# Twelve sums of token quarters moved from VectorE to GpSimd, with new slots for weight pieces and a new order in the first up iteration

## The reference

```
def conv_ffn(x, norm_g, w_up, conv_w, conv_b, w_down):
    h = rms_norm(x, norm_g)
    a, b = split(h @ w_up, 2, axis=-1)            # D_FF = 2816 columns each
    a = causal depthwise conv of width 3 over a, + conv_b
    return (silu(a) * b) @ w_down
...
for l in range(2):
    x = x + hybrid_mixer(x, ...)
    x = x + conv_ffn(x, ...)
return rms_norm(x, final_norm)
```

## Time and profile before

| | |
|---|---|
| median of three executions | 1598.31 us |
| profiled execution, its own time | 1598.63 us |
| its span, first to last instruction | 1596.8 us |
| TensorE matmul busy | 1581.9 us (99%) |
| TensorE weight load busy | 1399.0 us (88%) |
| VectorE busy | 1123.5 us (70%) |
| ScalarE busy | 741.4 us (46%) |
| GpSimd busy | 239.7 us (15%) |

### The profile page before, as it was taken

One profiled execution on the slowest core, in us unless ns is written; L12 is line 12 of the kernel. 1 busy time (PEld: TensorE's weight loads), 2 busy tenths in 40 slices (PEclk: granted clock), 3 DMA queues, 4 the chain that ended last, 5 costly groups with the idle time before them and its releaser, 6 DMA issues.

```text
span 1596.8 us, 22779 instructions
## 1 busy us (share of the span) xinstructions
PE 1581.9 (99%) x9174; PEld 1399.0 (88%) x9174; DVE 1123.5 (70%) x1252; ACT 741.4 (46%) x945; POOL 239.7 (15%) x253
## 2 busy tenths in 40 slices
PE   9999999999999999999999999999999999999998
PEld 7888888888888999999988888888888889999887
DVE  7267875785679787796873778658757887888422
ACT  5344334542356555653533533345423555556313
POOL 4000000000221222331330000000004102222120
PEclk9999999999999999999999999999999999999999
DMA  5342222223228788899223322221223488884222
GB/s 193 105 120 79 80 80 92 67 70 101 95 92 245 232 235 234 273 230 260 75 99 105 107 80 79 80 93 67 80 93 105 125 245 220 240 234 145 93 92 93
DMA packets 62308, 216.74 MB, mean 136 GB/s; under 512 B 6912, under 2 KB 7424, under 8 KB 62208
## 3 DMA queue, kind: packets, MB, share of 16 engines
q1 hardware_dynamic: 51408, 180.05, 33.0%
q0 software_dynamic: 8640, 30.41, 10.7%
q10 hardware_dynamic: 2160, 4.86, 1.1%
HBM read 211.10 MB, written 2.10 MB: 134 GB/s over the span
## 4 chain that ended last, share of the span: by engine, by line
PE 97%; DMA 2%; DVE 1%; issue 0%; ACT 0%; DVEq 0%
PE ps L1778 19%; PE ps L1780 19%; PE ps L1779 19%; PE ps L1784 11%; PE ps L1786 11%; PE ps L1785 11%; PE ps L1907 1%; PE ps L1896 1%; DMA w_raw<-wts 1%; PE ps L1874 1%; PE ps L1878 1%; DMA far_raw<-wdn 1%; PE ps L2031 0%; PE ps L1918 0%; PE ps L1844 0%
## 5 line engine op out<-in xcount | busy, mean ns | idle before, releaser
L1201 DVE TENSOR_TENSOR w_lo<-w_raw,w_hi 128x1024 fp32r<-128x1024 f32 x180 | 236.2, 1323 | 131.9 <-ACT w_hi L769 131.4
L1778 PE MATMUL ps<-u_hi,w_hi 128*128 128x512 f32 x768 | 301.5, 393 | 0.0
L1780 PE MATMUL ps<-u_hi,w_lo 128*128 128x512 f32 x768 | 299.2, 390 | 0.0
L1779 PE MATMUL ps<-u_lo,w_hi 128*128 128x512 f32 x768 | 299.1, 390 | 0.0
L769 ACT ACTIVATE w_hi<-w_raw 128x1024 fp32r<-128x1024 f32 x180 | 187.5, 1053 | 150.5 <-DMA w_raw<-wts 144.3
L1784 PE MATMUL ps<-comb_hi,far_hi 128*128 128x256 f32 x688 | 195.1, 284 | 4.1 <-DVE comb_lo L1411 2.4
L1785 PE MATMUL ps<-comb_lo,far_hi 128*128 128x256 f32 x688 | 194.7, 283 | 0.0
L1786 PE MATMUL ps<-comb_hi,far_lo 128*128 128x256 f32 x624 | 176.5, 283 | 0.0
L1780 PEld LDWEIGHTS ps<-u_hi,w_lo 128*128 128x128 f32 x768 | 144.2, 188 | 30.5
L1778 PEld LDWEIGHTS ps<-u_hi,w_hi 128*128 128x128 f32 x768 | 144.4, 188 | 28.4
L1779 PEld LDWEIGHTS ps<-u_lo,w_hi 128*128 128x128 f32 x768 | 144.4, 188 | 28.3
(11 more groups left out here) (311 smaller groups left out, 3294.7 us busy)
## 6 DMA issues: line engine op xcount, KB each, us to landing
w_raw<-wts SPq DMA_DIRECT2D x234, 512.0 KB, 3.5
far_raw<-wts SPq DMA_DIRECT2D x56, 512.0 KB, 3.7
w_raw<-wts POOLq DMA_DIRECT2D x18, 512.0 KB, 10.0
far_raw<-wts POOLq DMA_DIRECT2D x16, 512.0 KB, 7.0
t_raw<-wdn POOLq DMA_DIRECT2D x15, 512.0 KB, 9.9
w_raw<-wdn SPq DMA_DIRECT2D x11, 512.0 KB, 7.6
far_raw<-wdn SPq DMA_DIRECT2D x9, 512.0 KB, 7.4
first_raw<-wts SPq DMA_DIRECT2D x8, 512.0 KB, 6.4
```

What stands on the lines that cost most here:

```text
L1201: nc.vector.tensor_tensor(w_lo[:, s, :], w_raw[:, s, :], w_hi[:, s, :].bitcast(F32), ALU.subtract).then_inc(s_lo, 1)
L1778: nc.tensor.matmul(dst, a_hi, b_hi, start=start, stop=False)
L1779: nc.tensor.matmul(dst, a_hi, b_lo, start=False, stop=False)
L1780: return nc.tensor.matmul(dst, a_lo, b_hi, start=False, stop=stop)
```

## The change

- The twelve chunk_sum operations move from VectorE's program to GpSimd's, between the accumulating transfers: sums 3 to 8 (products 1 and 2) within the two rounds of add_piece for products 2 and 6, sums 12 to 14 (product 4) behind them and ahead of product 4's transfers, sums 15 to 17 (product 5) last. Their waits stay the same.
- RAW_SLOT is new from piece 19 on: product 3 takes slots 0, 2, FAR, FAR+1, FAR+2, FAR+3, and the following go round all eight slots in that manner. The order of SP's loads follows from it, and the waits of u_high for the last far slots are one piece earlier.
- In the first up iteration (n = 0, both layers): SP loads piece 5 behind pieces 2 and 6; ScalarE's last plain_tap moves from ahead of part_high 3 to behind part_high 4; VectorE's last plain_out moves from the end of the plain part to behind part_low(0, 2); its L1702 (now bottom_right) moves ahead of c11 and of part_low(1, 0).

```diff
--- before.py
+++ after.py
@@ -61,8 +61,8 @@
 CHUNKS = 21
 FAR = RING
 RAW_SLOT = [3, 1, 0, 2, FAR, FAR + 1, FAR + 2, FAR + 3, 3, 1, FAR + 2, FAR + 3, 3, 1, FAR + 2, FAR + 3, 3, 1,
-            0, FAR + 2, FAR + 3, 3, 1, 0, 2, FAR, FAR + 1, FAR + 2, FAR + 3, 3, 1, 0, 2, FAR, FAR + 1, FAR + 2,
-            FAR + 3, FAR, FAR + 1, FAR + 2, FAR + 3, FAR]
+            0, 2, FAR, FAR + 1, FAR + 2, FAR + 3, 3, 1, 0, 2, FAR, FAR + 1, FAR + 2, FAR + 3, 3, 1, 0, 2,
+            FAR, FAR + 1, FAR + 2, FAR + 3, FAR, FAR + 1]
 HI_SLOT = [(2, 1, 0, FAR, FAR + 1, FAR + 2, FAR + 3, 3)[u % 8] for u in range(39)] + [FAR, FAR + 1, 3]
 HI_AFTER = (0, 1, 2, 3, 4, 5, 6, 7)
 SUM_K = (1, 2, 4, 5)
@@ -585,10 +585,10 @@
                 load_part(l, 0, 3, W21, s_el[3])
                 sp.wait_ge(s_free, base + 2)
                 load_part(l, 0, 0, W11, s_el[0])
-                load_part(l, 0, 5, W22, s_el[5])
                 sp.wait_ge(s_free, base + 3)
                 load_part(l, 0, 2, W22, s_el[2])
                 load_part(l, 0, 6, W21, s_el6[0])
+                load_part(l, 0, 5, W22, s_el[5])
                 sp.wait_ge(s_free, base + 4)
                 load_part(l, 1, 1, W11, s_el1[1])
                 for n in range(SPLIT if l + 1 == DEPTH else SPLIT - 1):
@@ -703,12 +703,37 @@
                     pool.wait_ge(s_tland[int(j > 1)], l * (32 + 32 * (j > 1)) + 32 + 32 * (j > 1))
                     add_piece(l, j, W12)
 
+            def chunk_sum(l, c):
+
+                k, i = divmod(c, 3)
+                if k == 1:
+                    pool.wait_ge(s_gf, l * FT + HF + 4 * i + chunk(i))
+                    nc.gpsimd.tensor_tensor(chunk_raw(1, i), token_part(1, 1, i), token_part(0, 1, i), ALU.subtract).then_inc(s_csum, 1)
+                if k == 2:
+                    pool.wait_ge(s_csum, l * 12 + i + 1)
+                    pool.wait_ge(s_clo, l * CHUNKS + 3 + i + 1)
+                    nc.gpsimd.tensor_tensor(chunk_raw(2, i), chunk_raw(1, i), token_part(0, 0, i), ALU.add).then_inc(s_csum, 1)
+                if k == 4:
+                    pool.wait_ge(s_csum, l * 12 + i + 1)
+                    nc.gpsimd.tensor_tensor(chunk_raw(4, i), chunk_raw(4, i), token_part(0, 0, i), ALU.subtract).then_inc(s_csum, 1)
+                if k == 5:
+                    pool.wait_ge(s_csum, l * 12 + 3 + i + 1)
+                    pool.wait_ge(s_clo, l * CHUNKS + 6 + i + 1)
+                    nc.gpsimd.tensor_tensor(chunk_raw(5, i), chunk_raw(2, i), token_part(1, 0, i), ALU.subtract).then_inc(s_csum, 1)
+
             def further_sums(l):
 
+                chunk_sum(l, 3)
                 for k, quarter in ((1, W22), (2, W21)):
                     for j in range(PIECES):
+                        if k == 1 and j % 2 == 1:
+                            chunk_sum(l, 4 + j // 2)
+                        if k == 2 and j in (0, 2):
+                            chunk_sum(l, 7 + j // 2)
                         pool.wait_ge(s_qlo, l * UNITS_DOWN + k * PIECES + j + 1)
                         add_piece(l, j, quarter)
+                for c in (12, 13, 14):
+                    chunk_sum(l, c)
                 for j in range(PIECES):
                     u = 4 * PIECES + j
                     s = RAW_SLOT[u]
@@ -758,6 +783,8 @@
                 gated(l, SPLIT - 1)
                 if l + 1 < DEPTH:
                     further_sums(l)
+                    for c in (15, 16, 17):
+                        chunk_sum(l, c)
             sum_squares(DEPTH * 30, lambda k: DEPTH * TILES + k + 1, range(4))
 
         @block.scalar
@@ -956,7 +983,7 @@
                     act.wait_ge(s_tile, down_tile(l - 1) + 6)
                     for k in range(4, KT):
                         if k % 2 == 0:
-                            act.wait_ge(s_unit, (l - 1) * UNITS_DOWN + (40 if k == 4 else 41))
+                            act.wait_ge(s_unit, (l - 1) * UNITS_DOWN + (39 if k == 4 else 40))
                         u_high(k, pcol(l, PAR_ATTN + k))
                         if k % 2 == 1:
                             split_hi(l, k // 2 - 1)
@@ -1086,7 +1113,6 @@
                     done = 7 * (l * SPLIT + n)
                     if n == 0:
                         part_high(l, 0, 2)
-                        plain_tap(l, PLAIN - 1, 1)
                     else:
                         last_quarter(l, n - 1)
                         for h in range(2):
@@ -1097,6 +1123,8 @@
                         act.wait_ge(s_c11, l * SPLIT + n)
                     nc.scalar.activation(copy_x[:], half_tiles(banks(n)[0]), ACT.Copy).then_inc(s_cpx, 1)
                     part_high(l, n, 4)
+                    if n == 0:
+                        plain_tap(l, PLAIN - 1, 1)
                     act.wait_ge(s_prod, done + 2)
                     if n > 0:
                         act.wait_ge(s_c22, l * SPLIT + n)
@@ -1366,6 +1394,14 @@
                 dve.wait_ge(s_el6[n % 2], 16 * (l * ((SPLIT + 1 - n % 2) // 2) + n // 2 + 1))
                 nc.vector.tensor_tensor(part_raw(l, n, 6), part_raw(l, n, 6), part_raw(l, n, 2), ALU.add).then_inc(s_sum4, 1)
 
+            def bottom_right(l, n):
+
+                m = l * SPLIT + n
+                dve.wait_ge(s_prod, 7 * m + 5)
+                dve.wait_ge(s_cpy, m + 1)
+                dve.wait_ge(s_gf, l * FT + 2 * (PLAIN + n))
+                nc.vector.tensor_tensor(cb[:, :, S // 2:S], half_tiles(banks(n)[0]), copy_y[:], ALU.subtract).then_inc(s_c22, 1)
+
             def plain_out(l, g, h):
 
                 slab_done(l, UP0 + 4 * g + 2 * h + 1)
@@ -1409,24 +1445,6 @@
                     nc.vector.scalar_tensor_tensor(out=lo, in0=raw, scalar=-1.0, in1=hi, op0=ALU.mult, op1=ALU.subtract).then_inc(s_clo, 1)
                 else:
                     nc.vector.tensor_tensor(lo, raw, hi, ALU.subtract).then_inc(s_clo, 1)
-
-            def chunk_sum(l, c):
...
             def take_product(l, k):
 
@@ -1662,7 +1680,6 @@
                         if (g, j) == (1, 3):
                             third_sum(l, 0)
                             part_low(l, 0, 1)
-                            plain_out(l, g, 1)
                 for n in range(SPLIT):
                     m = l * SPLIT + n
                     a, b, c = banks(n)
@@ -1672,6 +1689,7 @@
                     if n > 0:
                         conv(l, 2 * (PLAIN + n) - 2)
                     else:
+                        plain_out(l, PLAIN - 1, 1)
                         comb_low(l, 4)
                     part_low(l, n, 3)
                     if n == 0:
@@ -1685,6 +1703,8 @@
                     part_low(l, n, 6)
                     if n == 0:
                         plain_gated(l, 2 * PLAIN - 1)
+                    if n == 0:
+                        bottom_right(l, 0)
                     dve.wait_ge(s_prod, 7 * m + 4)
                     dve.wait_ge(s_cpx, m + 1)
                     dve.wait_ge(s_c1, l * FT + 2 * (PLAIN + n))
@@ -1696,10 +1716,8 @@
                         chunk_low(l, 0)
                     else:
                         split_lo(l, DOWN0)
-                    dve.wait_ge(s_prod, 7 * m + 5)
-                    dve.wait_ge(s_cpy, m + 1)
-                    dve.wait_ge(s_gf, l * FT + 2 * (PLAIN + n))
-                    nc.vector.tensor_tensor(cb[:, :, S // 2:S], half_tiles(a), copy_y[:], ALU.subtract).then_inc(s_c22, 1)
+                    if n > 0:
+                        bottom_right(l, n)
                     if n + 1 < SPLIT:
                         third_sum(l, n + 1)
                     elif l + 1 < DEPTH:
@@ -1729,11 +1747,9 @@
                     if t == 0:
                         conv(l, FT - 2)
                         conv(l, FT - 1)
-                    c = (t + 3) // 2 if t % 2 == 1 else t // 2 + 2
+                    c = (t + 3) // 2
                     if t % 2 == 1 and c < CHUNKS:
                         chunk_low(l, c)
-                    if t % 2 == 0 and c < CHUNKS and c // 3 in SUM_K:
-                        chunk_sum(l, c)
                 for i in range(DOWN0, DOWN0 + FT if l + 1 == DEPTH else DOWN0):
                     c = i - DOWN0 + 3
                     if c < PAIRS:
```

More of the change, by code:

```diff
@@ L1411, in chunk_low @@
                     nc.vector.tensor_tensor(lo, raw, hi, ALU.subtract).then_inc(s_clo, 1)
-            def chunk_sum(l, c):
-                k, i = divmod(c, 3)
-                if k == 1:
-                    dve.wait_ge(s_gf, l * FT + HF + 4 * i + chunk(i))
-                    nc.vector.tensor_tensor(chunk_raw(1, i), token_part(1, 1, i), token_part(0, 1, i), ALU.subtract).then_inc(s_csum, 1)
-                if k == 2:
-                    dve.wait_ge(s_csum, l * 12 + i + 1)
-                    dve.wait_ge(s_clo, l * CHUNKS + 3 + i + 1)
-                    nc.vector.tensor_tensor(chunk_raw(2, i), chunk_raw(1, i), token_part(0, 0, i), ALU.add).then_inc(s_csum, 1)
-                if k == 4:
-                    dve.wait_ge(s_csum, l * 12 + i + 1)
```

(5 more changed lines are left out.)

## The result

The changed kernel takes 1605.33 us at the median of 5 runs (1599.50 to 1609.66) against 1598.31: ratio 1.0046, interval [1.0026, 1.0066]. It is slower by 7 us; the forecast was 1592.0 with a range of 1588 to 1599.5.

What follows compares the result with a forecast made beforehand. TensorE was taken to bound the kernel, busy 1581.9 of 1596.8 us, so only its stalls could be won. -5.4 (first up iteration) - 5.0 (slots) + 3.7 (sums) = -6.7 us from 1598.63, given as 1592.0, range 1588 to 1599.5.

Steps and rivals of the forecast that it cites:

- First up iteration: Both layers: reordering removes waits ahead of products 1, 2 and 6; gain 6.7 - 1.3 = 5.4 us, bounds 3.3 and 6.7.
- moving piece 5: First up iteration: piece 2 lands about 2 us sooner, so third_sum starts 0.55 and 1.4 us earlier in the two layers.
- New slots: Layer 0's down stage: loading product 3's pieces 18 to 21 ahead removes a 3.3 us stall and 1.7 of clock, 5.0 us.
- 1.4 us booked under the sums: Down stage, product 4: piece 24 ready at 745 to 747 us but due at 744.6; 1.4 us of loss taken.
- behind it the pieces follow as before, with 3 us in hand: Down stage, product 4: the pieces after piece 24 arrive with 3 us to spare, no loss charged.
- Sums: Down stage: twelve sums on GpSimd at 4.1 us (3.1 for 768) lose 1.2 + 1.1 + 1.4 = 3.7 us; bounds 0 and some 14.
- a sum there costs VectorE about 2 us where its own addition cost 1.14: Down stage: a GpSimd sum slows VectorE's operation beside it, as a pair stretched a subtraction from 1.23 to 2.34 us.
- had "10 us": Down stage, product 5: sums 15 to 17 have 10 us, no loss charged.
- each wait no longer than the 1.41 us that left the clock alone: Down stage: the sums' waits of 1.2, 1.1 and 1.4 us would not lower TensorE's clock.
- "Slower": Rival: sums of about 4.6 us make GpSimd's chain pace products 1 and 2, down stage costs 14 us, 1602.3 us; chance 0.14.
- "Clean": Rival: GpSimd sums take 2.6 to 3.2 us and their waits vanish, 1588.2 us; chance 0.18.
- The two waits worked out below would be gone: Down stage: at the skill's estimated 2.25 us a sum, the 1.2 and 1.1 us waits ahead of products 1 and 2 vanish.

Runs made afterwards that it cites:

- the second profile: Another profile of the unchanged changed kernel, nearer its median, span 1604.2 us; the changed kernel timed once more took 1606.05 us, ratio 1.0049.
- the faster one: The first profiled execution of the changed kernel, the fastest of its five runs, span 1597.7 us.
- the kernel with the sums alone: The kernel before with only the twelve sums moved to GpSimd, old slots and old orders: 1605.05 us, ratio 1.0048.
- the spare memsets: All sums on VectorE in the changed kernel, plus three GpSimd memsets of an unread tile in each of the twelve sum places: 1593.47 us, ratio 0.9974.
- the kernel with sums 12 to 17: The changed kernel with sums 3 to 8 back on VectorE and only 12 to 17 on GpSimd: 1599.60 us, ratio 1.0009.
- the first split sum: First sum in the changed kernel with every GpSimd sum issued as four (three) operations of 128x256: 1610.71 us, ratio 1.0086.

## Why the prediction was wrong

*First up iteration: right.* The gaps forecast to go went, in both layers, to about 0.45 us each where 0.6 was charged; 5.4 us forecast, 4.6 measured. (Twice 0.6 is 1.2 and not the 1.3 of the sum; it changes nothing.) One reason was half right: moving piece 5 showed a gain in layer 1's trace alone.

*New slots: wrong.* "The stall of 3.3 us and its 1.7 us of clock go: 5.0 us" held for the place and not for the time. The stall at 732 went, and product 4 took it over. Measured gain: 1.1 us on the kernel before (an interval that holds zero) and 1.2 behind the new orders (two intervals that overlap). The prediction named product 4 as the next late thing, but its piece 24, with 1.4 us booked under the sums, and "behind it the pieces follow as before, with 3 us in hand". With all sums on VectorE piece 24 is in time, and it is piece 26 behind it that is late: 2.17 us and 1.7 of clock at 748. That wait belonged to the slots, with an accumulating transfer of 12.59 us where 7.8 was taken.

*Sums: the step that failed* is "a sum there costs VectorE about 2 us where its own addition cost 1.14". It came from the earlier trace rows, a subtraction of 2.34 us beside two multiplications of 4.13, read as two engines that share and both slow down. The prediction took that one row as the price of any operation beside GpSimd's. Each sum is faster than assumed, 2.7 us, and costs VectorE up to all of that: the subtraction beside it takes 3.0 to 3.65 us. Worked out by the forecast's own sum for product 2: the low part of sum 6 was to last 2.2 us and end 1.1 us late; it lasts 3.60, behind low parts of 3.65, 3.07 and 3.37, and TensorE waits 3.24 us, where the forecast had 1.2 ahead of product 1 (none came there, and 0.27 ahead of its second piece) and 1.1 more ahead of product 2. The triples of sums were charged with no hold of VectorE at all: 12 to 14 entered only by delaying product 4's transfers, and 15 to 17 had "10 us". Sums 12 to 14 stretch a subtraction to 7.78 us, with 1.64 us of wait ahead of product 3; 15 to 17 stretch one to 8.24 us in the second profile, with 7.32 us of wait, and one to 2.62 in the faster one, with 2.88. The sums cost 13.4 us where 3.7 was forecast. By size the errors are 9.7 us for the sums, 3.8 for the slots and 0.8 for the orders: 14.3, against 1605.3 - 1592.0 = 13.3; the kernel before stood at 1598.31 in one comparison and 1597.74 in the other.

*The clock:* "each wait no longer than the 1.41 us that left the clock alone" fell with the waits. The one of 3.24 us took 1.7 us more with it in the changed kernel, though the same gap left the clock alone in the kernel with the sums alone.

*The rivals.* "Slower", 1602.3, came nearest in time, but by a mechanism that isn't there: it wanted sums of 4.6 us, and the spare memsets show that GpSimd's occupation by itself costs next to nothing. "Clean" was right that a sum takes 2.6 to 3.2 us and wrong that its waits would vanish: the two engines' times were treated as one question. In the prediction every fast sum was good news, and nothing in it priced a fast sum that stops VectorE.

The Trainium skill's page GPSIMD Engine Reference (section 1 Specifications and 4.1 Engine selection) was cited for the sharing and for an addition's place on VectorE. Its direction was right, and the measured 2.7 us stands between its estimated 2.25 and the 4.1 taken. "The two waits worked out below would be gone" held for the one ahead of product 1 and not for that of product 2, which came out at 3.24 us with the shorter sum.

*Open:* why product 4's piece 26 is in the air for so long (less traffic did not cure it); why sums cost 7.3 us on the old slots and 13.4 on the new ones (the old stall may have hidden a part); the kernel with sums, new orders and old slots wasn't run. Also what decides which engine stands: at 708.31 it was VectorE, at 716.50 of the kernel with sums 12 to 17 it was GpSimd, and the quarters of the first split sum took turns with VectorE. No run has one of the engines read a single SBUF operand beside the other's two.

The best of all kernels here is the changed one with its sums on VectorE: 1591.91 us, 0.9963 [0.9949, 0.9976]; the orders alone give 1593.12, and the two intervals overlap.

## What to carry to other kernels

Work moved from VectorE to GpSimd is not free because GpSimd is idle: if both read two SBUF operands, reckon with its whole duration on top of whatever VectorE does at that moment, and ask whether TensorE waits for that. Look in the trace for a VectorE operation whose end stands one own duration behind a GpSimd operation's end: one such row tells a hold from a slowdown, and a test with a result nobody reads costs one run. And where new slots bring one product's pieces sooner, the loads that they push back can be the next stall: price each of them, and not the first alone, in the same term.

## What the runs showed that was not expected

- A two-operand tensor_tensor on GpSimd (2.66 to 2.73 us for 128x1024) held VectorE's two-operand SBUF operation until it was over, and the reverse happened too: one sum took 5.95 us beside VectorE's subtractions of 1.22.
- The hold lasted over operations that follow each other: 7.78 us beside three sums (6.89), 8.78 beside eleven quarters (7.89). It did not always last: beside the four quarters of the first split sum (4.97) and beside sums 15 to 17 in the faster execution (8.19) VectorE got in.
- A memset on GpSimd held nothing: 1.22 us beside it.
- The clock fell to 0.57 behind gaps of 2.17 and 3.24 us and stayed at 1.00 behind 1.91, 2.88 and, in the kernel with the sums alone, behind another of 3.24; the length of a gap alone did not settle it here.
